# Expert 30's down projection moved between the two gate-up halves of expert 31

## What is computed

```python
gu = xb @ w_gate_up[eid] + b_gate_up[eid]
gate = jnp.minimum(gu[:, :D_FF], SWIGLU_LIMIT)
up = jnp.clip(gu[:, D_FF:], -SWIGLU_LIMIT, SWIGLU_LIMIT)
glu = gate * jax.nn.sigmoid(gate * SWIGLU_ALPHA)
return ((up + 1.0) * glu) @ w_down[eid] + b_down[eid]
```

## Time and profile before

| | us |
|---|---|
| three runs | 1021.88, 1022.59, 1022.75 (median 1022.59) |
| the profiled execution, its own time | 1022.09 |
| its span in the trace | 1020.3 |
| PE busy in the span | 998.4 |
| ACT busy, DVE busy | 149.9, 279.9 |
| bytes moved | 423.87 MB, 415 GB/s over the span |

### The profile page before, as it was taken

How to read it: one execution, slowest core, us unless ns; L and a number is a source line. 1 busy time by engine, 2 the same in 40 slices (tenths; PEclk the granted TensorE clock), 3 DMA queues, 4 the chain that set the end, 5 groups by cost and what they waited for, 6 DMA issues and landing times.

```text
span 1020.3 us, 12891 instructions
## 1 busy us (share of the span) xinstructions
PE 998.4 (98%) x5032; PEld 413.1 (40%) x5032; DVE 279.9 (27%) x685; ACT 149.9 (15%) x302; POOL 10.8 (1%) x29
## 2 busy tenths in 40 slices
PE   9999999999999999999999999999999999999997
PEld 7799733333333333333333333333333333333334
DVE  2888522222212221222221222212221221122122
ACT  2311311111111111111111111111111111111112
POOL 1010000000000000000000000000000000000000
PEclk9999999999999999999999999999999999999999
DMA  9986999999999999999999999999999999999996
GB/s 371 424 337 252 405 380 416 430 432 433 427 429 430 432 432 430 430 432 430 430 432 432 432 432 432 432 432 432 432 432 430 432 432 432 430 426 430 426 422 259
DMA packets 24662, 423.87 MB, mean 415 GB/s; under 512 B 3000, under 2 KB 3648, under 8 KB 7360
## 3 DMA queue, kind: packets, MB, share of 16 engines
q1 hardware_dynamic: 23616, 422.10, 97.3%
q10 hardware_dynamic: 1024, 1.47, 0.4%
HBM read 422.51 MB, written 1.05 MB: 415 GB/s over the span
## 4 chain that ended last, share of the span: by engine, by line
PE 80%; DMA 18%; SPq 1%; issue 1%; DVE 0%; ACT 0%; POOL 0%; ACTq 0%; PEldq 0%; DVEq 0%; POOLq 0%
PE bank L1867 33%; PE bank L1888 18%; DMA ring<-in_w_expert 14%; PE bank L1517 5%; PE bank L1726 4%; PE y L1931 4%; DMA ring<-in_w_down_last 4%; PE bank L1906 3%; PE y L1667 2%; PE bank L1802 1%; PE bank L1570 1%; PE bank L1509 1%; PE bank L1985 1%; PE bank L1912 1%; PE bank L1667 1%; SPq L599 1%
## 5 line engine op out<-in xcount | busy, mean ns | idle before, releaser
L1867 PE MATMUL bank<-ring,x_t 128*64 128x512 f32 x1984 | 447.3, 597 | 0.2 <-DVE x_t L1330 0.2
L1867 PEld LDWEIGHTS bank<-ring,x_t 128*64 128x64 f32 x1984 | 134.1, 136 | 262.8 <-issue 259.3
L1888 PE MATMUL bank<-ring,act 128*64 128x512 f32 x960 | 223.0, 596 | 7.4 <-DMA ring<-in_w_expert 7.4
L1370 DVE TENSOR_TENSOR gu_b<-bank,bias_t 128x512 f32<-128x512 f32 x64 | 44.3, 692 | 323.5 <-PE bank L1906 323.4
L1888 PEld LDWEIGHTS bank<-ring,act 128*64 128x64 f32 x960 | 66.3, 137 | 133.5 <-issue 133.5
L836 ACT COPY gu_sb<-bank 128x512 f32<-128x512 f32 x64 | 37.5, 586 | 222.7 <-PE bank L1867 222.7
L1323 DVE TENSOR_TENSOR x_t<-bank,cols 128x512 f32<-128x512 f32 x30 | 20.7, 691 | 165.1 <-PE bank L1802 165.1
L1931 PE MATMUL y<-z,p_t 64*128 64x512 f32 x240 | 59.6, 615 | 0.0
L1726 PE MATMUL bank<-x_sb,p_row 128*64 128x512 f32 x248 | 58.5, 592 | 0.0
L1309 DVE TENSOR_SCALAR p_row<-slot,rank,rstd 128x64 f32<-128x64 f32 x62 | 16.6, 312 | 147.6 <-PE bank L1912 147.6
L840 ACT ACTIVATE act<-gu_b 128x256 f32<-128x256 f32 x62 | 25.8, 417 | 192.1 <-DVE gu_b L1376 192.1
(11 more groups left out here) (275 smaller groups left out, 537.7 us busy)
## 6 DMA issues: line engine op xcount, KB each, us to landing
ring<-in_w_expert SPq DMA_DIRECT2D x72, 4096.0 KB, 30.7
ring<-in_w_expert SPq DMA_DIRECT2D x34, 2048.0 KB, 15.1
ring<-in_w_expert SPq DMA_DIRECT2D x14, 1024.0 KB, 8.7
ring<-in_w_in SPq DMA_DIRECT2D x4, 2048.0 KB, 25.7
ring<-in_w_down_last SPq DMA_DIRECT2D x6, 1024.0 KB, 40.9
ring<-in_w_out SPq DMA_DIRECT2D x2, 2048.0 KB, 26.8
ring<-in_w_expert SPq DMA_DIRECT2D x8, 512.0 KB, 5.0
ring<-in_w_in SPq DMA_DIRECT2D x2, 1024.0 KB, 12.5
```

What stands on the lines that cost most here:

```text
L1370: dve.tensor_tensor(gu_b[:, :, :, :], bank[2][:, :].rearrange("p (f a s) -> p a f s", a=2, f=4), bias_t[:, :, 4 * h:4 * h + 4, ds(e, 1)] . ...
L1867: ins = mm(bank[h][a * SLOTS:(a + 1) * SLOTS, :], x_t_of(it)[:, k, :], w[:, kk, a, :], start=k == 0, stop=k == KT - 1)
L1888: ins = mm(bank[0][a * SLOTS:(a + 1) * SLOTS, :], act_of(it)[:, k, :], w[:, kk, a, :], start=k == 0, stop=k == KT - 1)
```

## The change

It loads and uses the down weights of expert 30 between the two gate-up halves of expert 31: chunks (30, 4) and (30, 5) now come before (31, 2) and (31, 3). It cuts expert 31's down chunks anew and loads the five parts alternately, chunk 4 first half, chunk 5 first half, chunk 4 second half, chunk 5 third quarter, chunk 5 last quarter. PE uses them in that order. Both experts now use bank 3 for half 0 and bank 0 for half 1.

```diff
 PIECES = {(E - 1, 3): HALVES, (E - 2, 4): HALVES, (E - 2, 5): HALVES,
-          (E - 1, 4): (0, 2 * BY_K, 4 * BY_K, 8 * BY_K), (E - 1, 5): (0, 2 * BY_K, 6 * BY_K, 8 * BY_K)}
+          (E - 1, 4): HALVES, (E - 1, 5): (0, 4 * BY_K, 6 * BY_K, 8 * BY_K)}
+LAST_PIECES = ((4, 0), (5, 0), (4, 1), (5, 1), (5, 2))
...
-    order += [(it, j) for it in (E - 2, E - 1) for j in range(4)]
-    return order + [(it, j) for it in (E - 2, E - 1) for j in range(4, ITEM_CHUNKS)]
+    order += [(E - 2, j) for j in range(4)] + [(E - 1, j) for j in range(2)]
+    return order + [(E - 2, j) for j in range(4, ITEM_CHUNKS)] + [(E - 1, j) for j in range(2, ITEM_CHUNKS)]
...
-        return place_in_order(it, j) + 1
+        return place_in_order(it, j) + 1 - (2 if it == E - 1 and j >= 2 else 0)
...
-        HALF_BANK = {E - 2: (0, 3), E - 1: (1, 0)}
+        HALF_BANK = (3, 0)
...
-                        ends = PIECES[it, j]
-                        for p in range(len(ends) - 1):
+                        pieces = [(j, p) for p in range(len(PIECES[it, j]) - 1)]
+                        if it == E - 1 and j >= 4:
+                            sp.wait_ge(s_used, LAST + ITEM_CHUNKS - RING)
+                            pieces = LAST_PIECES if j == 4 else ()
+                        for j, p in pieces:
+                            ends = PIECES[it, j]
...
-                for h in range(2):
-                    keep_gate_up(b, h)
-                    sigmoid(b, h)
+                keep_gate_up(b, 0)
+                sigmoid(b, 0)
                 act_e.wait_ge(s_dna, 1)
-                act_e.copy(z[:, 0:QUARTER], bank[0][:, 0:QUARTER]).then_inc(s_za, 1)
+                act_e.copy(z[:, 0:QUARTER], bank[HALF_BANK[0]][:, 0:QUARTER]).then_inc(s_za, 1)
                 act_e.wait_ge(s_dn, a + 1)
-                act_e.copy(z[:, QUARTER:HALF], bank[3][:, 0:QUARTER]).then_inc(s_z, 1)
+                act_e.copy(z[:, QUARTER:HALF], bank[HALF_BANK[1]][:, 0:QUARTER]).then_inc(s_z, 1)
+                keep_gate_up(b, 1)
+                sigmoid(b, 1)
                 last_item()
...
                 gate_up(b, 1, range(4))
-                gate_up(b, 2, range(0, 2))
+                pe.wait_ge(s_av, 2 * b)
+                pe.wait_ge(s_ptk, b + 1)
+                down_half(a, 0, range(4))
                 turn(b, 0)
-                gate_up(b, 2, range(2, 4))
-                gate_up(b, 3, range(4))
-                pe.wait_ge(s_av, 2 * b)
-                down_half(a, 0, range(4))
-                turn(b, 1)
                 down_half(a, 0, range(4, KT)).then_inc(s_dna, 1)
-                pe.wait_ge(s_ptk, b + 1)
                 down_half(a, 1, range(4))
                 pe.wait_ge(s_za, 1)
                 scatter_half(a, 0, None)
                 down_half(a, 1, range(4, KT)).then_inc(s_dn, 1)
 
+                gate_up(b, 2, range(0, 2))
+                pe.wait_ge(s_z, b)
+                scatter_half(a, 1, s_y)
+                gate_up(b, 2, range(2, 4))
+                gate_up(b, 3, range(4))
                 pe.wait_ge(s_av, 2 * b + 1)
                 down_half(b, 0, range(0, 2))
-                pe.wait_ge(s_z, b)
-                scatter_half(a, 1, s_y)
+                turn(b, 1)
                 down_half(b, 0, range(2, 4))
+                down_half(b, 1, range(4))
                 pe.wait_ge(s_av, 2 * b + 2)
                 down_half(b, 0, range(4, KT)).then_inc(s_dnl, 1)
-                down_half(b, 1, range(0, 2))
+                down_half(b, 1, range(4, 6))
                 pe.wait_ge(s_zl, 1)
                 scatter_half(b, 0, s_yl)
-                ins = down_half(b, 1, range(2, KT))
+                ins = down_half(b, 1, range(6, KT))
```

More of the change, by code:

```diff
@@ L885, in last_item @@
                 act_e.wait_ge(s_dnl, 1)
-                act_e.copy(z[:, 0:QUARTER], bank[1][:, 0:QUARTER]).then_inc(s_zl, 1)
+                act_e.copy(z[:, 0:QUARTER], bank[HALF_BANK[0]][:, 0:QUARTER]).then_inc(s_zl, 1)
                 act_e.wait_ge(s_yl, 2)
@@ L892, in last_item @@
                 act_e.wait_ge(s_dn, E)
-                act_e.copy(z[:, QUARTER:HALF], bank[0][:, 0:QUARTER]).then_inc(s_z, 1)
+                act_e.copy(z[:, QUARTER:HALF], bank[HALF_BANK[1]][:, 0:QUARTER]).then_inc(s_z, 1)
             for it in range(LOOP_FROM):
@@ L1984, in down_half @@
                     for a in range(2):
-                        ins = mm(bank[HALF_BANK[it][h]][a * SLOTS:(a + 1) * SLOTS, 0:QUARTER], act_of(it)[:, k, :], w[:, k, a, :],
+                        ins = mm(bank[HALF_BANK[h]][a * SLOTS:(a + 1) * SLOTS, 0:QUARTER], act_of(it)[:, k, :], w[:, k, a, :],
                                  start=k == 0, stop=k == KT - 1)
```

## The result

| | kernel before | changed kernel |
|---|---|---|
| runs | 20 | 20 |
| median, us | 1022.47 | 1023.57 |
| lowest and highest, us | 1021.53, 1023.64 | 1022.51, 1026.12 |
| profiled execution, span, us | 1022.09, 1020.3 | 1024.0, 1022.2 |

The ratio is 1.0015, with a 95% interval of 1.0008 to 1.0022: the changed kernel is 1.1 us longer at the median, a small loss, but one that the interval separates from none. The forecast of the median was 1023.9.

The account below looks back on a forecast made before the run. In the last 35 us, PE and the DMA weight stream were taken to run side by side. PE's 0.7 us plus ACT's 0.65 made 1.35 us slower, 1023.9 us on the median, range 1021.9 to 1025.4.

Parts of the forecast that it names:

- What bounds: Weight stream and PE run side by side in the last 35 us; PE can win only its waits, 1.5 us.
- busy without a gap: Before the change, after a 0.54 us wait at 997.78, PE was said never to idle until its last scatter.
- The wait at gate-up (31, 2): In expert 31, PE is ready before chunk (31, 2) lands at 995.1 and waits 1.3 us.
- The wait of 0.4 us for the second half of (31, 4): In down (b, 0), PE is ready at 1007.7 but that part is usable only at 1008.1: 0.4 us.
- ACT's 0.65 us: At the end, copy z starts behind ACT's squares, 2.69 us after scatter (b, 0), instead of waiting for PE: 0.65 us.
- The items costed at nothing: Added load wait, ACT's copies, activation, table load and new bank numbers were all said to be covered, costing 0.
- SP's added wait: Issue of (31, 4) must wait until (29, 5) has been used; costs nothing, with 15 us of cover.
- The table load: ACT's 1.28 us load behind the last sigmoid ends near 1008, is needed near 1010, and costs nothing.
- The sum: Whole kernel: 0.7 us of PE plus 0.65 of ACT make it 1.35 us slower, 1023.9 on the median.
- rival (A): DMA waits nearly vanish; from 0.3 us less to 0.95 us more, 1022.3 to 1023.5; chance 0.22.
- Rival (C): PE's clock falls in the new wait, slowing eight gate-up instructions by 1.9 us, giving 1025.8; chance 0.02.
- (B): Parts around (31, 2) land at the slow spacing of 2.75 us: 3.25 us slower, 1025.8; chance 0.13.

Follow-up runs that it names:

- sixth kernel: Kernel before, with PE also waiting for the first part of (31, 3) before gate-up (31, 2): 1025.28 us, ratio 1.0029.
- fifth: The changed kernel run once more without an edit, also called the repeat: 1023.67 us, ratio 1.0017.
- third kernel: Changed kernel with only expert 30's down weights moved, the last parts cut and ordered as before the change: 1026.03 us, ratio 1.0028.
- first kernel: Changed kernel with chunk (31, 2) loaded in two parts of 1 MB: 1023.46 us, ratio 1.0008.
- tenth: Changed kernel with the last parts as before the change and 16 unused transposes in the wait before gate-up (31, 2): 1024.25 us, ratio 1.0017.
- ninth kernel: Changed kernel with ACT's two squares of half 0 cut to 8 columns instead of 256: one profiled execution, 1022.34 us.
- seventh: Changed kernel with PE also waiting for the first part of (31, 3) before gate-up (31, 2): 1027.54 us, ratio 1.0051.
- 8: Changed kernel with (30, 4) and (30, 5) loaded whole, two DMAs of 2 MB instead of four of 1 MB: 1023.20 us, ratio 1.0008.
- second kernel: Changed kernel with 16 unused transposes put where PE waits for (31, 2): 1023.85 us, ratio 1.0012.

## Why the prediction was right, and where it was not

**What bounds.** Right: PE after 892.40 follows the stream, and the halves, the filling and the whole loads moved the waits about and left the end in place. The list of waits was one short: "busy without a gap" from 997.78 on missed some 0.2 us inside the row of 32 at 1004.53, where PE takes up the second half of (31, 4) at its landing (3.80 us to the next row; the same row takes 3.61 in the sixth kernel). A reordering could thus win 1.7 us, not 1.5, and the step of 3.80 us that the forecast used for 32 instructions contains this wait.

**The wait at gate-up (31, 2).** The place was right, the size was not: 1.3 us forecast, 2.67, 2.51 and 2.47 measured (changed, fifth and third kernel). This is the term that was mis-sized. Counted from the landing of (31, 1), (31, 2) landed after 15.6 us, not 14.9, and PE was free after 13.0, not 13.7, since it stood 0.6 us nearer to the stream in this execution than in that of before (4.0 against 4.5 us between the landing of (31, 1) and PE's start on what follows). In the repeat the four parts took 10.0 us as forecast, (31, 2) then 5.3 instead of 4.86, and PE was free after 12.8. I had taken PE's position from one execution and the landings from a mean, and the difference of two such numbers is less certain than either.

**The wait of 0.4 us for the second half of (31, 4).** It came, with some 0.3 us, inside the row of 48. This is the wait that decides when the scatter starts; where the first wait is removed it shows as 0.59 us. So the sum of the DMA waits was 3.0 instead of 1.7. The error in the first wait did not carry through to the time, because PE would have waited at this landing instead, as the first kernel shows.

**ACT's 0.65 us.** The mechanism was right, the size was not: 0.4 us. z started 2.59 us after the scatter, 2.69 forecast, without waiting for PE, and PE alone would have let it start at 2.19, where the forecast had PE done at 2.0. PE's wait grew from 0.56 to 0.95 us in every kernel with the alternating parts and whole squares, and stayed at 0.56 in the third and tenth, which have the old parts. The ninth kernel shows the bound by taking it away.

**The items costed at nothing.** SP's added wait cost nothing: SP came to it at 971.46, 15 us after PE had used (29, 5). The table load ended at 1008.76 and was needed at 1010.76, and PE took up the second half of (31, 4) at its landing, not at the end of the activation. With the last parts in their old order the activation is no longer covered: 1.29 us in the third and tenth kernels.

**The sum.** 1.35 us forecast for the profiled execution, 1.9 measured, and 1.1 in the repeat. Of z's 1.84 us in the first, PE's down that ends 1.45 us later (1012.58 + 1.08 against 1009.40 + 2.81) has 1.45 where 0.7 was forecast, and ACT 0.4 where 0.65 was; in the repeat PE has 0.7. So one pair of executions differs by more than the errors of the terms. At the median it is 1.1 us. Without the upper group, by the 13 runs of the lower one, it is 0.8, which lies in the band of rival (A) although the waits did not vanish; why the lower group is some 0.3 us better than the repeat's profile (1023.19 against 1022.09) is open. The forecast of 1023.9 is 0.3 above the median of 1023.57, but partly by luck: that median is a mixture, a lower group 0.6 us better than I said and an upper one that I had nearly ruled out.

**Rival (C), the clock, given 0.02.** By the times it happens in 12 of 31 runs. Its price was right: 1.9 us forecast, 1.7 in the profile of the third kernel, 1.9 and 2.4 between the medians of the two groups. The step that failed is the evidence against it. I argued from a wait of 1.78 us that left the clock at 1.00, and that I expected only 1.3. The true wait was 2.5 to 2.7, and no row of before showed a PE idle for so long. A row clears only waits up to its own length. (The Trainium skill, TensorE: Matmul & The Clock Gate, section HAM oscillation, says that waits for a DMA can throttle the array again. The windows of the third and seventh kernels agree, with 0.50 and 0.59.) In the changed kernel itself the fallen clock was not caught in a profile. That its upper group is this is inferred from the third kernel's profile, from the kernels without the long wait or with it filled (1, 2 and 8: none of 33 runs above 1024.5), and from the sixth, which has only the wait.

**Rivals (A) and (B).** No profile had (A): the waits did not vanish. (B), the slow spacing throughout, did not come either; but one part, the second half of (30, 5), did land 3.4 us after the one before it (988.04 and 991.43), slower than the 2.75 I took as the slowest.

## What to carry to other kernels

Where an engine follows a stream that bounds it, measure each order against a landing that no order has moved, and look for the landing behind which the end always starts at the same distance. The waits ahead of that one are only bookkeeping, and a new order of loads is judged by how late it makes that one. But the shape of the waits still matters, because one long wait can cost clock where three short ones don't; so cut loads or place other work such that PE never idles long before a dense stretch. And look at all times of a kernel, not at the median alone, since two groups with a gap point to a mechanism that one profile may miss.

## What the runs showed of the hardware

- **Behind a PE wait of 2.47 us and behind one of 4.33 us the granted clock was 0.50, and behind waits of 2.51, 2.63, 2.67 and 2.90 us in other profiles it stayed at 1.00.** By the groups of times it is chance from run to run: 12 of 31 runs of the changed kernel, 5 of 8 of the third, 5 of 7 of the sixth (2.90 us), all 5 of the seventh (4.33 us). Behind waits up to 1.78 us no profile shows it.
- **16 transposes, 2 us of PE time, in the idle stretch kept the clock up** in all 11 runs of the second kernel, as far as the times tell, and in its profile. In the tenth the five runs at 0.996 are gone too, though two of its 11, at 1025.05 and 1025.30, can't be told from a small loss of clock.
- **A landing can come late while the bytes flow at full rate.** From 980.56 to 991.43 the four 1 MB parts landed, 4.19 MB; the window of this stretch says 427 GB/s, which is 4.64 MB. The rest must have belonged to loads issued later. In the repeat the same four parts landed in 9.97 us at 426 GB/s, 4.25 MB:

```profile
980.56:991.43 10.87, 10.87 (x80) 5.72 (x78) 2.04 (x5) 1.75 (x4) 0.00 (x0) 1.00 1.03 427
```

  The Trainium skill, DMA: Bandwidth & Descriptors, section "Why a DMA increments its semaphore by 16 and not by 1", says that the engines of one DMA finish independently and that all must have landed. That fits, but no run here shows the single engines. For an estimate it means that a mean rate can give landings that are 1 us too early.
